# The same program with its on-chip tiles at other addresses

## The reference, cut to what matters

```python
def swiglu(x, w1, w3, w2):
    h = jax.nn.silu(jnp.einsum('btd,df->btf', x, w1)) * jnp.einsum('btd,df->btf', x, w3)
    return jnp.einsum('btf,fd->btd', h, w2)

def expert_block(args):              # one block of 128 chosen tokens, one expert
    xb, e = args
    h = jax.nn.silu(xb @ w1[e]) * (xb @ w3[e])
    return h @ w2[e]
```

## Time and profile before

| | us |
|---|---|
| median of 3 runs | 2278.28 |
| lowest and highest of them | 2276.2, 2283.25 |
| span of the profiled execution | 2280.6 |
| TensorE busy in it | 2201.9 (97%) |
| share of TensorE in the chain that ended last | 91% |

### The profile page before, as it was taken

One profiled execution on the slowest core, in us unless ns is written; L12 is line 12 of the kernel. 1 busy time (PEld: TensorE's weight loads), 2 busy tenths in 40 slices (PEclk: granted clock), 3 DMA queues, 4 the chain that ended last, 5 costly groups with the idle time before them and its releaser, 6 DMA issues.

```text
span 2280.6 us, 32139 instructions
## 1 busy us (share of the span) xinstructions
PE 2201.9 (97%) x12243; PEld 1836.9 (81%) x12243; DVE 1554.8 (68%) x1678; ACT 1178.6 (52%) x1194; POOL 170.5 (7%) x242
## 2 busy tenths in 40 slices
PE   8989999998899999999999999999899999999998
PEld 7877887897778888888888888888688878877886
DVE  3655453465488888989898988888765426867453
ACT  4133442313266767767676767677564322355442
POOL 1200000320300000000000000000075010200000
PEclk9999999999899999999999999999999999999999
DMA  9124555412389999999999999999756554425552
GB/s 344 58 93 130 186 184 184 138 58 93 109 294 364 343 361 344 352 345 356 343 357 340 356 364 343 359 346 353 263 166 189 171 148 146 149 80 170 184 184 74
DMA packets 251028, 537.26 MB, mean 236 GB/s; under 512 B 18006, under 2 KB 140928, under 8 KB 250560
## 3 DMA queue, kind: packets, MB, share of 16 engines
q1 hardware_dynamic: 246800, 521.11, 65.1%
q0 software_dynamic: 3168, 9.07, 1.7%
q10 hardware_dynamic: 976, 5.91, 0.6%
HBM read 534.71 MB, written 1.31 MB: 235 GB/s over the span
## 4 chain that ended last, share of the span: by engine, by line
PE 91%; DVE 5%; ACT 2%; issue 1%; DMA 0%; DVEq 0%; SPq 0%; ACTq 0%
PE bank L1359 9%; PE bank L1363 9%; PE bank L1360 9%; PE bank L1232 9%; PE bank L1234 9%; PE bank L1233 8%; PE bank L984 6%; PE bank L1485 5%; PE bank L1379 5%; PE bank L1375 5%; PE bank L1374 5%; PE bank L1175 2%; PE bank L1334 1%; DVE arena L2418 1%; PE bank L1347 1%
## 5 line engine op out<-in xcount | busy, mean ns | idle before, releaser
L2215 DVE TENSOR_TENSOR weights_lo<-ring_data,weights_hi 128x2048 fp32r<-128x2048 f32 x336 | 759.2, 2288 | 99.5 <-ACT weights_hi L1927 98.7
L1927 ACT ACTIVATE weights_hi<-ring_data 128x2048 fp32r<-128x2048 f32 x336 | 636.1, 1917 | 173.3 <-DMA ring_data<-in_moe_w 172.5
L1359 PE MATMUL bank<-weights_hi,xg_hi 128*128 128x512 f32 x896 | 357.2, 399 | 4.0 <-DVE arena L2625 2.6
L1360 PE MATMUL bank<-weights_hi,xg_lo 128*128 128x512 f32 x896 | 352.5, 393 | 0.0
L2210 DVE TENSOR_TENSOR weights_lo<-ring_data,weights_hi 128x2048 fp32r<-128x2048 f32 x98 | 227.2, 2349 | 52.3 <-ACT weights_hi L1714 52.3
L1363 PE MATMUL bank<-weights_lo,xg_hi 128*128 128x512 f32 x896 | 243.8, 393 | 0.0
L1233 PE MATMUL bank<-weights_lo,xT_hi 128*128 128x512 f32 x584 | 227.9, 390 | 0.0
L1232 PE MATMUL bank<-weights_hi,xT_hi 128*128 128x512 f32 x520 | 208.0, 400 | 1.2 <-DVE xT_lo L2203 0.6
L1234 PE MATMUL bank<-weights_hi,xT_lo 128*128 128x512 f32 x520 | 203.8, 392 | 0.0
L1359 PEld LDWEIGHTS bank<-weights_hi,xg_hi 128*128 128x128 f32 x896 | 168.3, 188 | 42.5 <-issue 3.0
L1363 PEld LDWEIGHTS bank<-weights_lo,xg_hi 128*128 128x128 f32 x896 | 168.3, 188 | 40.6
(11 more groups left out here) (462 smaller groups left out, 3200.8 us busy)
## 6 DMA issues: line engine op xcount, KB each, us to landing
ring_data<-in_moe_w SPq DMA_DIRECT2D x672, 512.0 KB, 4.3
ring_data<-in_ffn_w_in SPq DMA_DIRECT2D x88, 512.0 KB, 4.8
ring_data<-in_w_in SPq DMA_DIRECT2D x70, 512.0 KB, 4.7
ring_data<-in_ffn_w SPq DMA_DIRECT2D x66, 512.0 KB, 4.1
ring_data<-in_ffn_w_out SPq DMA_DIRECT2D x44, 512.0 KB, 3.9
ring_data<-in_w_out SPq DMA_DIRECT2D x24, 512.0 KB, 4.5
ring_data<-in_w_in SPq DMA_DIRECT2D x8, 396.0 KB, 4.2
ring_data<-in_w_in SPq DMA_DIRECT2D x8, 390.0 KB, 5.7
```

The costliest lines, as they stand in the source:

```text
L1359: mm(o, xg_hi[:, k, :], e_hi(at)[:, r], start=k == 0, stop=False)
L1360: mm(o, xg_lo[:, k, :], e_hi(at)[:, r], start=False, stop=False)
L1927: nc.scalar.activation(e_hi(at), ring_data[:, e_slot(at), :], ACT.Copy).then_inc(ring.hi_done, 1)
L2215: v.tensor_tensor(e_lo(at), ring_data[:, e_slot(at), :], e_hi(at), ALU.subtract).then_inc(ring.lo_done, 1)
```

## The change

The order in which tiles are allocated is another, and filling tiles are put between them so that the big ones start at multiples of 512 bytes. By the arithmetic of `sb` the first bytes are:

| tile | before | modulo 512 | after | modulo 512 |
|---|---|---|---|---|
| consts_sb | 16512 | 128 | 16640 | 256 |
| ring_data | 31904 | 160 | 44544 | 0 |
| x | 81056 | 160 | 93696 | 0 |
| actT | 89248 | 160 | 101888 | 0 |
| lnp | 97440 | 160 | 110080 | 0 |
| prow | 105632 | 160 | 43520 | 0 |
| params | 106656 | 160 | 32256 | 0 |
| headg | 112896 | 256 | 38496 | 96 |
| small | 113920 | 256 | 39520 | 96 |
| arena | 118048 | 288 | 118272 | 0 |
| Y_lo, in params | 108384 | 352 | 33280 | 0 |

So the three tiles that the 512-column matmuls read most stand at 160, 160 and 288 modulo 512 before and all at 0 after; modulo 64 all three stand at 32 before. `cln` moves up in `params`, on the host as in the kernel, so that `Y_lo` too starts at a multiple of 512. `arena` loses 24 words and `small` 24 words that nothing used. Every engine has the same instructions in the same order with the same waits; only addresses (and line numbers) differ.

```diff
-ARENA = 27672
+ARENA = 27648
+SMALL = 1000
+CONSTS_AT, PARAMS_AT, RING_AT = 130 * 128, 63 * 512, 87 * 512
-PARAMS = {"pcol": (DEPTH, P), "hpar": (DEPTH, 24), "nrmw": (DEPTH, HD), "cln": (DEPTH, 2, CW), "router": (DT, E), "lncol": (2, 2, DT), "memg": (DT,)}
+PARAMS = {"pcol": (DEPTH, P), "cln": (DEPTH, 2, CW), "hpar": (DEPTH, 24), "nrmw": (DEPTH, HD), "router": (DT, E), "lncol": (2, 2, DT), "memg": (DT,)}
+    parts += [every(v[k][l]) for l in range(DEPTH) for k in ("cnv_ln_g", "cnv_ln_b")]
     for l in range(DEPTH):
         parts += [every(v[k][l]) for k in ("gdn_dt_bias", "fox_f_bias", "gdn_a_log")] + [np.zeros((P, 6), np.float32)]
     parts += [every(v["gdn_norm_w"][l]) for l in range(DEPTH)]
-    parts += [every(v[k][l]) for l in range(DEPTH) for k in ("cnv_ln_g", "cnv_ln_b")]
+        def from_here(at):
+            gap = at - (nc.sbuf_base + 31) // 32 * 32
+            if gap < 0 or gap % 4:
+                raise ValueError((at, nc.sbuf_base))
+            if gap:
+                ctx.enter_context(nc.sbuf_tensor(f"gap{at}", [P, gap // 4], F32))
+        npass_i = sb("npass_i", [P, 2], I32)
+        from_here(CONSTS_AT)
         consts = sb("consts_sb", [P, CONST_W])
+        from_here(PARAMS_AT)
+        params = sb("params", [P, PARAM_W])
...
+        headg = sb("headg", [P, 4, HD])
+        toep = nc.dram_tensor("toep", (AH, 16, 512), F32, kind="Internal").ap()
+        small = sb("small", [P, SMALL])
+        prow = sb("prow", [P, DEPTH, P])
+        from_here(RING_AT)
         ring_data = sb("ring_data", [P, RING, 8 * FC])
         x = sb("x", [P, TT, D])
         actT = sb("actT", [P, DT, T])
         lnp = sb("lnp", [P, 2, D])
-        prow = sb("prow", [P, DEPTH, P])
-        params = sb("params", [P, PARAM_W])
...
-        headg = sb("headg", [P, 4, HD])
-        toep = nc.dram_tensor("toep", (AH, 16, 512), F32, kind="Internal").ap()
-        small = sb("small", [P, 1024])
-        npass_i = sb("npass_i", [P, 2], I32)
         arena = sb("arena", [P, ARENA])
```

More of the change, by code:

```diff
@@ L331, in two_block_kernel, with param @@
         ident, ones, half = const("ident"), const("ones"), const("half")
+        from_here(PARAMS_AT)
+        params = sb("params", [P, PARAM_W])
+        def param(k):
+            o, *dims = PARAM_AT[k]
+            return shaped(params[:, o:o + int(np.prod(dims))], *dims)
+        pcol, cln, hpar, nrmw, router_sb, lncol, memg = (param(k) for k in PARAMS)
+        headg = sb("headg", [P, 4, HD])
[3 more added lines that the diff above has]
+        from_here(RING_AT)
         ring_data = sb("ring_data", [P, RING, 8 * FC])
@@ L374, in __call__ @@
                 self.at += n
-                if self.at > 1024:
+                if self.at > SMALL:
                     raise ValueError(self.at)
```

## The result

The median is 2254.12 us over four runs (2251.73 to 2257.1) against 2278.97 for the kernel before (2276.2 to 2283.25). The ratio is 0.9891, interval 0.9878 to 0.9903: 25 us, 1.1% faster. The forecast was no change.

The account below looks back on a forecast made before the run. TensorE was taken to bound the kernel. 2280.6 us plus 2 us for the 512-column matmuls and 0 for the rest gave 2282.6 us profiled, 2280 us as median; own range 2271 to 2285, whole range 2207 to 2297.

Parts of the forecast that it names:

- The count of 6,576 matmuls: 512-column matmuls on the path: 4,032 in the experts and 2,544 in the dense layers, 1,519 us at present.
- 215.8 and 233.3 ns: Bounds for the 512-column distance: plain matmul's 215.8 ns, 100 us less; slowest steady pattern's 233.3 ns, 15 us more.
- The reading that two reads of TensorE: 512-column matmuls: reads of moving and next stationary operand meet again and again, losing 15 ns each time.
- The doubt that the start modulo 64 matters: Against 64-byte starts being faster: moving operands in consts_sb start at a multiple of 64 and are slower.
- Rival A: 512-column matmuls: the loss shrinks or goes; 33 us less at 226 ns, 87 at 215.8 ns; chance 0.36.
- by the nearest rows: 512-column matmuls after the change: 231.3 ns taken from steps whose operands already stood alike; 2 us more.
- two patterns: Experts' down step, same tiles: five matmuls 226 ns apart, eight 232.5 apart; more than one pattern possible at one set of addresses.
- another wait as the sign that TensorE outruns what feeds it: Experts' part: should TensorE outrun the loads, its waits for ScalarE appear there; no size given.
- Rival B: 512-column matmuls: with equal phases the slow pattern of the dense down step holds everywhere; 15 us more, 2293 us; chance 0.28.
- C: 512-column matmuls: distances come from their order alone, nothing depends on these addresses; 2278 us; within the forecast's chance of 0.36.
- rows 7 and 9: Dense up step, moving hi operand at 288 and 128 modulo 512: nine matmuls in 2.06 and 2.10 us, 228.9 and 233.3 ns each.
- The first wait: TensorE's 8.4 us wait for a DMA at the start; 1/17 of it, 0.5 us, was estimated from the extra transaction.

Follow-up runs that it names:

- the actT runs: Kernel after with actT and lnp moved to 32, 64, 128, 192 or 224 modulo 256: 2281.71, 2284.37, 2280.50, 2261.63 and 2279.43 us.
- all160: Kernel after with the ring and all behind it moved by 160 bytes: 2257.89 us, ratio 0.9913 to the kernel before.
- arena128: Kernel after with arena alone moved up by 128 bytes: 2281.27 us, ratio 1.0007 to the kernel before.

## Why the prediction was wrong

**What held.** TensorE bounds the kernel, and its 512-column matmul is the place. No other engine's time moved: VectorE 2,289 ns as forecast, copies and parameters nothing. The count of 6,576 matmuls holds, and 215.8 and 233.3 ns did bound the mean. The reading that two reads of TensorE, of the moving and of a stationary operand, cost the time between them was right (the actT runs); that it is the next stationary operand is not shown. The doubt that the start modulo 64 matters was right too (all160). Rival A is what happened, near its price for 226 ns: 33 us forecast, 25 measured.

**What failed is one step: the value taken for the distance when both operands stand alike.** The prediction took 231.3 ns, "by the nearest rows": hi weights and hT stand alike in `arena`, and the down steps with them were at 233.3 and 231.2. The runs show 226.7 for operands that stand alike. The nearest rows were not, taken whole, a case of equal phase. In a triple of the dense down step hi stood alike with hT, but the lo weights in `ring_data` at 160 did not stand alike with hT at 288, and so it is with a third of the matmuls of the experts' down step. The prediction took the phase of a pair for what decides a matmul; in fact a pair out of phase throws off the pattern for its neighbours too. arena128 shows this best: there the hi weights and hT are at one phase, as before, only lo isn't, and 233.3 ns comes back (for the hT triples of that run the starts give 235.7, 234.0 and about 230 ns, all three above 226.7).

The two stretches of the experts' down step do lie at equal phase, each within eight matmuls of hi weights with hT, and the prediction took 226 and 232.5 ns for two patterns that may hold there. The starts tell another story. From 807.80 on the kernel before has 235, 233, 236, 224, 231, 236, 228, 233 ns: the sequence with which the kernel after begins when it comes out of a pause, cut off by the lo weights at its eighth matmul. The slot at 743.47 comes into it near its end, with 231, 233, 231 ns, and has 226 and 227 from 744.17 until the lo weights:

```profile
743.47 0.39 PE L1374 MATMUL bank<-weights_hi,hT_hi 128*128 128x512 f32 x1
```

Of 96 such slots without a pause, 40 end at 226 and 227 ns in the kernel before and the others are still on the way; in the kernel after all 96 are there from their first matmul. So the steady value at equal phase stood in the rows (226 by the rows, 226.6 by the starts), and 232.5 was what comes before it. Rows at equal phase that differ should have been taken as a question of what stood beside them.

**Sizes.** Averages over all starts of the trace: experts 231.7 to 227.1 ns, 4,032 x 4.6 = 18.5 us; dense down triples 700.7 to 680.2 ns, 264 x 20.5 = 5.4 us; dense up triples 686.7 to 681.8, 584 x 4.9 = 2.9 us. Together 26.8. Given back: 2.4 us at the second scatter. That leaves 24.4 of the 25.3 us between the two spans; what is left, 0.9 us, lies outside these matmuls and is less than the runs of one kernel differ by. Rival A's 33 us were 6 too many in the mean distance (about 227 over all, not 226.0; the steady value is 226.7, and after a pause the pattern takes up to nine matmuls to settle) and 2.4 in the new wait. The prediction had named another wait as the sign that TensorE outruns what feeds it, one for ScalarE; this one is for VectorE's additions of the scatter before.

**Rival B** had the right cause the wrong way round: equal phase is the best place found, not the slowest. **C** is out: arena128 and the kernel after have one order of matmuls, and 231.6 and 227.0 ns.

**Two readings to put right.** The granted clock is not 0.9 or more in every slice: one slice, around 600 us, is at 0.8. No 512-column matmul of the sum lies there, so the sum stands. And rows 7 and 9 don't have the same stationary tiles: `xT_lo` lies in `arena` in the first block and over `lnp` in the second. That is not what makes their difference, for in the second block the triples with hi weights from `arena` have the same distances as in the first, 232, 226 and 228 ns in the mean, some 687 for a triple, of which three fill the 2.06 us of rows 7. It does show that a mix of phases is not priced pair by pair: `xT_lo` stands at another phase there and nothing changes.

**Two rules, and the loads.** The Trainium skill ("SBUF — State Buffer") says under "Who interferes with whom" that TensorE has two independent read ports and waits on nobody. These runs disagree as far as float32r matmuls go: 226.7 ns at one phase of stationary to moving operand, 229 to 234 at five others. The Trainium skill ("DMA: Bandwidth & Descriptors", "How a descriptor splits into AXI transactions") says that a descriptor that starts off a multiple of 256 bytes has its first transaction start at the boundary below. For the 4 KB rows of the prediction that is one transaction more; a short one can do without. The DMA issues of the kernel after (ring at 0), then of the one with the ring at 160:

```profile
ring_data<-in_moe_w SPq DMA_DIRECT2D x672, 512.0 KB, 4.3
...
ring_data<-in_w_in SPq DMA_DIRECT2D x70, 512.0 KB, 4.5
```

```profile
ring_data<-in_moe_w SPq DMA_DIRECT2D x672, 512.0 KB, 4.4
...
ring_data<-in_w_in SPq DMA_DIRECT2D x70, 512.0 KB, 4.8
```

For `in_w_in` the direction agrees in every run: 4.5 to 4.6 us in the eleven with the ring at 0, 4.7 to 4.8 in the three with it at 160, the kernel before among them. For `in_moe_w` it is 4.2 to 4.3 against 4.3 to 4.4, which hardly tells. The first wait, from which the prediction worked out an estimate of 0.5 us by that section of the Trainium skill, doesn't show it: 8.4 us before, 8.3 after, and 8.2 with the ring at 160 again. The rest is hidden behind TensorE, as forecast.

## What to carry to other kernels

Where matmuls of 512 float32r columns fill the time, read the distance of their starts, not their duration, and set it against that of a plain matmul in the same trace. If it is over 226.7 ns, try to let stationary and moving operands start at the same address modulo 256, all of them: one kind of pair out of step cost its neighbours too, and 128 bytes of filling were worth 1% here. And when rows at "the same" setting differ, find what stands beside and before them, and read the single distances in order, before taking their mean.

## What the runs showed of the hardware

- The distance between two 512-column float32r matmuls depends on the address of the stationary operand less that of the moving one, modulo 256: 226.7 ns at 0, 229.5 at 192, 232.6 to 233.8 at 32, 64, 128 and 224 (experts' up step). Moving the ring and all behind it by 160, or `arena` by 256, leaves it as it is.
- At equal phase it settles at 226.7 ns; otherwise it runs through patterns between 224 and 242 ns that are the same from turn to turn. After a pause it needs up to nine matmuls to settle: 235, 233, 236, 224, 231, 236, 228, 233, 231 ns, then 226 and 227.
- A load of 64 stationary columns takes 134 ns and one of 128 columns 188, but shorter loads did not make the matmuls come faster at these addresses (229.2 ns).
- Plain float32 matmuls of 256 columns stay at 215.8 ns a record at every phase tried: the chain has 20.72 us for 96 of them with `actT` and the ring alike, before and after, and also in all five actT runs. The kernel after, and the run with `actT` at 128:

```profile
16.21 20.72 PE bank L997 x96
```

```profile
15.91 20.72 PE bank L999 x96
```
